# A hybrid decoder step on one core: where the residual's squares are summed, and the order of three pipelines

## The reference

```python
# layer 0: attention and convolution; layer 1: RWKV-7 time mixing
h = h + mix(rmsnorm(h, norm_mix[l]))
f = rmsnorm(h, norm_ffn[l])
h = h + (silu(f @ w_gate[l]) * (f @ w_up[l])) @ w_down[l]      # inner width 2816
# after both layers
y = rmsnorm(h, norm_final)
# rmsnorm(x, g) = x * rsqrt(mean(x * x) + eps) * g

# the end of the time mixing: ys is the state's output, 16 heads of 64
yn = (ys - mean(ys)) * rsqrt(var(ys) + GN_EPS) * lnx_g + lnx_b   # per head
out = ((yn + bonus) * g) @ rwkv_wo                               # g = sigmoid(xg @ g1) @ g2
```

## Time and profile before

| | |
|---|---|
| median of 3 executions | 3728.64 us (3728.14 to 3729.97) |
| profiled execution, whole | 3730.17 us |
| its span | 3728.4 us |
| TensorE busy | 3406.7 us, 91% |
| VectorE, ScalarE, GpSimd busy | 1154.4, 908.2, 460.2 us |
| granted TensorE clock, mean | 0.949 |

### The profile page before, as it was taken

The page is one execution under the profiler, slowest core; times in us unless marked ns, Lnnn a source line. Parts: engine busy times, 40 slices in busy tenths (PEclk is TensorE's granted clock), DMA queues, the critical chain, the costliest instruction groups (busy, mean ns, idle before and its releaser), DMA issues. The chain is left out here.

```text
span 3728.4 us, 65930 instructions
## 1 busy us (share of the span) xinstructions
PE 3406.7 (91%) x29166; PEld 2836.6 (76%) x29166; DVE 1154.4 (31%) x1968; ACT 908.2 (24%) x1542; POOL 460.2 (12%) x375
## 2 busy tenths in 40 slices
PE   5999687879999999979999699998899799999996
PEld 3667354559999999946555399998455799999995
DVE  1099653131111111151445333433232311112112
ACT  2001234122111111110245333332252311111111
POOL 0000110001122122100011111110000122122120
PEclk9999898889999999989999799999589899999998
DMA  2123342111111111112032322221300111111111
GB/s 79 51 49 96 123 159 92 34 34 40 46 49 48 37 54 46 35 35 87 31 135 104 124 45 55 51 46 50 122 0 1 46 41 51 42 52 49 37 46 61
DMA packets 171994, 222.35 MB, mean 60 GB/s; under 512 B 104739, under 2 KB 122916, under 8 KB 170692
## 3 DMA queue, kind: packets, MB, share of 16 engines
q1 hardware_dynamic: 159284, 174.42, 15.8%
q0 software_dynamic: 12432, 43.80, 3.3%
HBM read 180.63 MB, written 37.55 MB: 59 GB/s over the span
## 5 line engine op out<-in xcount | busy, mean ns | idle before, releaser
L2415 PE MATMUL f_out<-f_u_hi,f_weights_hi 128*128 128x352 f32 x2112 | 685.4, 325 | 48.0 <-DVE f_u_lo L2457 48.0
L2416 PE MATMUL f_out<-f_u_lo,f_weights_hi 128*128 128x352 f32 x2112 | 680.4, 322 | 0.0
L2417 PE MATMUL f_out<-f_u_hi,f_weights_lo 128*128 128x352 f32 x2112 | 679.9, 322 | 0.0
L2391 POOL TENSOR_TENSOR f_weights_lo<-f_weights,f_weights_hi 128x1024 fp32r<-128x1024 f32 (+2 forms) x168 | 323.1, 1924 | 1731.2 <-ACT f_weights_hi L2427 1731.2
L2415 PEld LDWEIGHTS f_out<-f_u_hi,f_weights_hi 128*128 128x128 f32 x2112 | 399.2, 189 | 50.2 <-issue 40.8
L1292 PE MATMUL rf_out<-rf_mixed,rf_weights 128*128 128x352 f32 (+2 forms) x1344 | 413.7, 467 | 24.0 <-DVE rf_mixed L1451 24.0
L2416 PEld LDWEIGHTS f_out<-f_u_lo,f_weights_hi 128*128 128x128 f32 x2112 | 399.7, 189 | 0.0
L2417 PEld LDWEIGHTS f_out<-f_u_hi,f_weights_lo 128*128 128x128 f32 x2112 | 398.7, 189 | 0.0
L1292 PEld LDWEIGHTS rf_out<-rf_mixed,rf_weights 128*128 128x128 f32 (+2 forms) x1344 | 246.9, 186 | 185.7 <-issue 49.6
L2415 PE MATMUL f_out<-f_inner_hi,f_weights_hi 128*128 128x352 f32 x1056 | 341.4, 323 | 4.0 <-DVE f_inner_lo L2488 4.0
L2480 DVE TENSOR_TENSOR f_product<-f_out,f_gate 128x352 f32<-128x352 f32 x132 | 69.3, 525 | 880.3 <-PE f_out L2417 880.3
(11 more groups left out here) (348 smaller groups left out, 4467.7 us busy)
## 6 DMA issues: line engine op xcount, KB each, us to landing
f_weights<-in_w_gu SPq DMA_DIRECT2D x88, 512.0 KB, 3.5
f_weights<-in_w_down SPq DMA_DIRECT2D x48, 256.0 KB, 2.6
rf_weights<-in_w_rkv SPq DMA_DIRECT2D x24, 512.0 KB, 3.6
f_weights<-in_w_down SPq DMA_DIRECT2D x32, 320.0 KB, 2.9
all_hT<-in_x SPq DMA_DIRECT2D x2, 4224.0 KB, 13.0
all_hT<-in_cache_k SPq DMA_DIRECT2D x32, 256.0 KB, 4.7
all_hT<-in_cache_k POOLq DMA_DIRECT2D x32, 256.0 KB, 4.3
all_hT<-in_cache_v SPq DMA_DIRECT2D x32, 256.0 KB, 3.6
```

The lines of the kernel that those rows point to most:

```text
L2391: pool.tensor_tensor(lo[:, s, :w], raw[:, s, :w], hi[:, s, :w].bitcast(F32), ALU.subtract).then_inc(lo_ready, 1)
L2415: pe.matmul(out, hi[:, s, w], x_hi, start=(k == 0), stop=False)
L2416: pe.matmul(out, hi[:, s, w], x_lo, start=False, stop=False)
L2417: last = pe.matmul(out, lo[:, s, w], x_hi, start=False, stop=(k == parts - 1))
```

## The change

- Sums of squares: the stages of `inverse_rms` and of the final `rms_norm` are gone. A class `ResidualNorm` squares each piece (tile and chunk) of the residual on ScalarE once it is final, adds the squares up elementwise on VectorE in one tile `total`, and needs one product with the ones per chunk. It is used in `add_projection`, in `finish_heads` and in the last eight down jobs of `ffn_layer`. `rstd` is a tile of the whole program.
- The first two feed-forward jobs go chunk by chunk in turn, and the first waits piece by piece.
- The final norm scales `hT` in place and stores each chunk once it is scaled.
- In `finish_heads` ScalarE takes the Ln of each unit and, after each fourth, four Exp; buffers are longer, and gates, norm and projection are moved to later steps. Each tile of the bonus has a semaphore of its own.

```diff
+class ResidualNorm:
+    def square(self, act, x):
+        m, n = self.order[x]
+        y = self.adds[x]                      # pieces with m > 0 before x
+        if m and y >= 2:
+            act.wait_ge(self.added, y - 1)
+        dst = self.sq[:, y % 2] if m else self.total[:, chunk(n)]
+        act.activation(dst, self.hT[:, m, chunk(n)], ACT.Square).then_inc(self.squared, 1)
+    def add(self, dve, x):
...
+        dve.wait_ge(self.squared, x + 1)
...
+        dve.tensor_tensor(total, self.sq[:, y % 2], total, ALU.add).then_inc(self.added, 1)
+    def total_sum(self, pe, n, bank):
+        pe.wait_ge(self.added, self.end[n])
+        pe.matmul(bank[:, :TC], self.K.ones, self.total[:, chunk(n)], start=True, stop=True)...

 # finish_heads
-    LAG = KD + 3
+    GATE, NORM, LAG = GROUP, GROUP + 1, KD + GROUP + 2        # GROUP = 4
 # TensorE, step s
                     if s < UNITS_:
                         mean_sum(s)
-                    if 0 <= s - 1 < UNITS_:
-                        gates(s - 1)
+                    if 0 <= s - GATE < UNITS_:
+                        gates(s - GATE)
                     if s >= LAG:
                         project(s - LAG)
                     if 0 <= s - 1 < UNITS_:
                         var_sum(s - 1)
+                    if s == UNITS_ + LAG - 2:
+                        pe.wait_ge(q_["centred"], UNITS_)
+                        for n in range(NCH - 1):
+                            norm_.total_sum(pe, n, sum_banks[n])
 # ScalarE, step s
+                    if s + 1 < UNITS_:
+                        square(s + 1)
+                    if s < UNITS_:
+                        log(s)
+                        if s % GROUP == GROUP - 1:
+                            for u in range(s - GROUP + 1, s + 1):
+                                root(u)
+                    if s > LAG:
+                        act.wait_ge(q_["added"], s - LAG)
+                        norm_.square(act, s - LAG - 1)
 # VectorE, step s
                     if s + 1 < UNITS_:
                         centre(s + 1)
-                    if s >= LAG:
-                        add(s - LAG)
-                    if s < UNITS_:
-                        norm(s)
+                    if s > LAG:
+                        add(s - LAG - 1)
+                    if 0 <= s - NORM < UNITS_:
+                        norm(s - NORM)
+                    if s > LAG + 1:
+                        norm_.add(dve, s - LAG - 2)

 # ffn_layer
+                for n in range(NCH):
+                    for i in range(2):
+                        project(i, n)
+                for i in range(2, len(jobs)):
                     for n in range(NCH):
-                        if i == 0:
-                            pe.wait_ge(u_lo, (n + 1) * KD)
+                        project(i, n)        # in it: if i == 0: pe.wait_ge(u_lo, n * KD + k + 1)
 # ScalarE, behind the split of job i + 2
+                    if i >= final:
+                        for n in range(NCH):
+                            act.wait_ge(evacuated[i % 2], (i // 2) * NCH + n + 1)
+                            norm.square(act, t * NCH + n)
 # VectorE, behind each addition of the last eight down jobs
+                            if i >= final and x:
+                                norm.add(dve, x - 1)

+def final_norm(nc, hT, rstd, gain, out):
...
+                for n in range(NCH):
+                    sp.wait_ge(normed, n + 1)
+                    sp.dma_start(out[:, :, chunk(n)], hT[:, :, chunk(n)]).then_inc(stored, 16)
```

More of the change, by code:

```diff
@@ L2285, with _ @@
 FF_RING = 6
[L2288 to L2293, removed]
-        with nc.Block() as block:
[L2295 to L2300, removed]
-                for n in range(NCH):
-                    act.wait_ge(summed, KD)
-                    act.activation(rstd[:, chunk(n)], sums[n][:, :TC], ACT.Ln, scale=1.0 / D,
-                                   bias=K.norm_eps).then_inc(logged, 1)
-                for n in range(NCH):
[L2306 to L2316, removed]
+def final_norm(nc, hT, rstd, gain, out):
+    with Stage(nc, "nfin") as st:
+        normed, stored = st.sem("normed"), st.sem("stored")
+        with nc.Block() as block:
+            @block.vector
+            def _(dve):
+                for n in range(NCH):
+                    for k in range(KD):
+                        op = dve.scalar_tensor_tensor(hT[:, k, chunk(n)], hT[:, k, chunk(n)], gain[:, k:k + 1],
+                                                      rstd[:, chunk(n)], ALU.mult, ALU.mult)
+                    op.then_inc(normed, 1)
+            @block.sync
+            def _(sp):
+                for n in range(NCH):
+                    sp.wait_ge(normed, n + 1)
+                    sp.dma_start(out[:, :, chunk(n)], hT[:, :, chunk(n)]).then_inc(stored, 16)
+                sp.wait_ge(stored, 16 * NCH)
 class FfnJobs:
@@ L2364, in ffn_layer, with done @@
         normed, u_hi, u_lo, f_hi, f_lo = (st.sem(n) for n in ("normed", "u_hi", "u_lo", "f_hi", "f_lo"))
+        LAST = len(jobs) - 1
+        final = len(jobs) - KD
+        def done(i, n):
+            return 2 * n + i + 1 if i < 2 else i * NCH + n + 1
         def width(job):
@@ L2395, in _, with project @@
             def _(pe):
-                for i, (kind, t, g) in enumerate(jobs):
+                def project(i, n):
+                    kind, t, g = jobs[i]
                     s = i % 2
-                    pe.wait_ge(lo_ready, i + 1)
-                    if i >= 2:
+                    if n == 0:
+                        pe.wait_ge(lo_ready, i + 1)
+                    if i >= 2 and n == 0:
                         pe.wait_ge(evacuated[s], (i // 2) * NCH)
-                    if kind == "down":
+                    if kind == "down" and n == 0:
@@ new lines, in project @@
+                    parts = KD if kind != "down" else FF_GROUPS[g]
+                    for k in range(parts):
+                        if i == 0:
+                            pe.wait_ge(u_lo, n * KD + k + 1)
+                        w = slice(k * P, (k + 1) * P)
+                        if kind == "down":
+                            at = (order.group_tiles[g].start + k) % FF_RING
+                            x_hi, x_lo = fh[:, at, chunk(n)], fl[:, at, chunk(n)]
+                        else:
+                            x_hi, x_lo = uh[:, k, chunk(n)], ul[:, k, chunk(n)]
+                        pe.matmul(out, hi[:, s, w], x_hi, start=(k == 0), stop=False)
+                        pe.matmul(out, hi[:, s, w], x_lo, start=False, stop=False)
+                        last = pe.matmul(out, lo[:, s, w], x_hi, start=False, stop=(k == parts - 1))
@@ L2489, in _ @@
                                               fh[:, t % FF_RING, chunk(n)].bitcast(F32), ALU.subtract).then_inc(f_lo, 1)
+                norm.add(dve, KD * NCH - 1)
 def program(nc, A, O):
```

179 lines of the change are left out of this document (113 added, 66 removed).

## The result

| | before | after |
|---|---|---|
| median | 3728.4 us (4 runs, 3722.8 to 3730.0) | 3704.8 us (4 runs, 3701.1 to 3711.4) |
| profiled execution's span | 3728.4 us | 3709.5 us |
| granted TensorE clock, mean | 0.949 | 0.942 |

The ratio is 0.9943, with a 95% interval of 0.9928 to 0.9959: 15 to 27 us faster, where 30 were forecast. By the traces three parts gained 86 us between them and the heads' stage lost 61.5.

What follows compares the result with a forecast made beforehand. TensorE, busy 91% of the span, was taken as the bound, so only its standing still could be won. Terms -59.4 - 18.0 - 5.9 + 53 = -30.3 us took 3728.64 to 3698 us, range 3655 to 3714.

Steps and rivals of the forecast that it cites:

- Norms: Four norms: squares and additions move under products, leaving a 6.2 us ScalarE chain at each; gain 59.4 us, between 52 and 62.
- Squares at nothing: Squares and additions under the output projection and last down jobs priced at no cost; without cover, 16 us a layer.
- The Exp behind its load: In the norms, Exp starts right behind its 1.28 us table load; the skill's 1.38 us drain would cut 11 us of gain.
- First feed-forward jobs: First two gate jobs alternate by chunk, 9.0 us gained a layer (ends 6 and 10), 18.0 us in two layers.
- Last norm: Final norm stores each chunk once scaled, the last store taking 5.5 us; gain 5.9 us, between 3 and 8.
- Heads' stage: Heads' last stage loses 53 us, ends +10 and +74, despite fewer table loads.
- The ring: Heads' stage: mean, centre, norm, gates, var, next mean wait in a circle each step; 8.08 us half clock, 5.25 full.
- +74 (two falls a step): Upper end of the heads' stage loss, if TensorE's clock falls twice in each projecting step.
- (a): Rival: clock holds through gaps of the heads' projecting steps, head stays at half; loss 38, total 3683; chance 13%.
- (b): Rival: full clock in the heads' head too; stage loss 10, total 3655; chance 10%.
- (c): Rival: no ring binds, head goes at TensorE's 5.6 us a step, stage some 10 us earlier; total 3635; chance 7%.
- (d): Rival: clock never recovers inside the ring, projecting steps 18.2 us, stage loss 116, total 3761; chance 4%.

Runs made afterwards that it cites:

- experiment 5: Changed kernel with gates a step later, plus one unused Ln ahead of the last squares at each norm to load the table early: 3601.7 us, ratio 0.9668.
- experiment 7: Changed kernel with gates a step later, squaring and adding only residual tiles 0 and 7 of eight (norms wrong, timing only): 3596.3 us, ratio 0.9658.
- experiment 1: Changed kernel with the gates of the heads' last stage issued one step later: 3598.9 us, ratio 0.9653, stage 184.1 us.
- experiment 2: Changed kernel with VectorE's norm operations placed ahead of centre in each step of the heads' stage: 3608.5 us, ratio 0.9671, stage 188.1 us.
- experiment 3: Changed kernel with three unused TensorE products added ahead of the gates in steps 6 to 23 of the heads' stage: 3650.8 us, stage 236.3 us.
- experiment 8: Changed kernel with one unused TensorE product added ahead of the gates in steps 6 to 23 of the heads' stage: 3671.7 us, stage 257.6 us.

## Why the prediction came out as it did

The forecast was 3698 us; 3704.8 were measured. All its mechanisms were found. The gains came out 2.5 us larger than forecast and hid part of a loss that was 8.5 us larger.
- **Norms**, 59.4 forecast, 58.6 measured. Three gaps are the 6.2 us of the sum; the third is 7.1, since the stage behind it starts later: its releaser is L155, the barrier behind the clearing of finished stages' semaphores, which the prediction had named for this place. The chain on ScalarE was right as a sum of rows, but it is not ScalarE's alone: experiment 5 shows that taking the load of 1.28 us away wins only 0.4 to 0.6 us.
- **Squares at nothing**: right (experiment 7).
- **The Exp behind its load**: it starts 0.02 us behind the end of the load (797.02 + 1.28 to 798.32), and so before the change, where the load ahead of 809.43 is this:

```profile
808.14 1.28 ACT L2307 ACT_TABLE_LOAD   x1
```

  The drain that the Trainium skill ("ScalarE: Activation LUTs", "What ACT_TABLE_LOAD costs") adds to each switch is not in the trace; by it each gap would have been 9.0 us.
- **First feed-forward jobs**, 18.0 forecast, 21.1 measured. The late stall that I named is there, a wait of 0.84 us for GpSimd's low part at job 2; I had priced it and the loss at half clock some 1.5 us too high a layer.
- **Last norm**, 5.9 forecast, 6.1 measured.
- **Heads' stage**, +53 forecast, +61.5 measured. The ring is the cause (experiments 1 and 2), its head step of 8.08 us is the one worked out, and the free tail of 81 us is too. The mis-sized term is the clock in the nine ringed projecting steps: I took one fall of 3.4 us at half clock, 1.7 us a step, from the one place where the trace of before showed such a fall. It lasted 6.6 us here (2709.80 to 2716.40) and cost 3.1, by experiment 3. 9 x 1.5 = 13 us more, of which the head gave back 3 by reaching its first projection after 83.1 us instead of 86, and what follows the ring some 2. Of the ends, +74 (two falls a step) doesn't come out of these terms: nine more falls of 1.7 give 68, which is what the range goes by.
- **Rivals.** (a) is out: half clock stood in each of the projecting steps. The Trainium skill ("TensorE: Matmul & The Clock Gate", "Why this matters for your kernels") warns of gaps longer than any of these, and 2.79 us were enough each time; experiment 8 shows 2.20 us going both ways. (b), full clock throughout, is what experiment 3 made by force: 9.7 us more than before in the stage, where the working gave 10. (c) and (d) are out: 46.8 us of waiting at the gates, and a clock that comes back in every step. A stage in which no ring binds is that of experiment 1; (c) had put it some 10 us below the old one, and it came 42.5 below.

What I didn't see ahead is on the other side: that the head's half clock wasn't given. I took 5.6 us, its work at half clock, as TensorE's pace there. At full clock it is 2.75, and the same stage is done in 184 us. The rows that show this stood in the trace of before: TensorE ran at full clock by 2664.28, then waited 4.54 us, most of it for VectorE's wait of 4.26 us for the load of the bonus, and stood at half clock in the rest of the head:

```profile
2664.28 0.76 PE L2168 MATMUL hw_mean<-c_yT,all_constants 128*128 128x352 f32 x2
...
2668.30 0.58 DVE L2247 SCALAR_TENSOR_TENSOR hw_centred<-hw_centred,all_vectors,hw_bonus 128x352 f32<-128x352 f32 x1 [4.26 <-DMA hw_bonus<-scratch_bonus]
...
2669.57 1.54 PE L2182 MATMUL hw_gate<-c_lora,hw_gate 128*128 128x352 f32 x2 [4.54 <-DVE c_yT L2251]
```

## What to carry to other kernels

When an order is stretched so that a slow step gets distance, write down for each pair of waits in how many steps it comes back to itself: a wait that closes within one step sets the step's length, however far the rest is stretched, and here one number or one swap opened it. Price what TensorE loses by standing still twice, as the gap and as the half clock behind it: here the two cost 52 us each. If a stage runs at half clock, look for the wait behind which the clock fell, and for short waits behind it, before taking its pace for a limit.

## What the runs showed of the hardware that was not expected

- Work that is thrown away made the changed kernel's stage 52 us shorter (288.1 to 236.3): with 54 more products in TensorE's gaps the clock stayed up.
- Two heads with nearly the same gap run at different clocks. In the kernel with the old order TensorE waits 0.92 us in each step and stays at half clock, to which it came behind a wait of 3.54 us that ends at 2636.87; in the kernel with single logarithms it waits 0.87 us, came to it out of a dense stretch, and stays at full clock. The stretches of the two, in that order:

```profile
2640.00:2680.00 40.00, 33.74 (x49) 12.86 (x49) 12.74 (x24) 25.25 (x31) 0.00 (x0) 0.50 0.04 16
```
```profile
2630.00:2647.00 17.00, 13.13 (x35) 5.34 (x36) 9.30 (x17) 16.75 (x22) 0.00 (x0) 1.00 0.17 69
```

By busy time the one at half clock is the busier (33.74 of 40 us, 13.13 of 17), but its instructions also take twice as long; by their number it does less (49 in 40 us, 35 in 17). It may be that such a wait keeps a clock down or leaves it up by where it came from; the two heads differ in their orders too, and no run was made to test that alone.
